# The last rows of an MLP: two products share banks, six half blocks leave VectorE, a pause in GpSimd's transfers

## What is computed

```python
proj = jnp.einsum('bsd,dc->bsc', x, w_in)          # 512 x 1024 times 1024 x 7680
y_a, y_b, y_c = conv(...), hgrn2(...), memory_attention(...)
merged = (sigmoid(ga + b_ga) * (y_a @ w_branch[0])
          + sigmoid(gb + b_gb) * (y_b @ w_branch[1])
          + sigmoid(gc + b_gc) * (y_c @ w_branch[2]))
x = layer_norm(ALPHA * x + merged @ w_o, ln1_g, ln1_b)
h = square(relu(x @ w_up))                          # 512 x 4096
x = layer_norm(ALPHA * x + h @ w_down, ln2_g, ln2_b)   # ALPHA = 2 ** 0.25
```

## Time and profile before

| | |
|---|---|
| median of three runs | 813.63 us (812.73 to 814.42) |
| the profiled execution | 814.37 us, of which the span from first to last instruction is 812.6 us |
| TensorE busy | 800.1 us (98%), granted clock 0.997 |
| VectorE, ScalarE, GpSimd busy | 552.5, 402.6, 117.2 us |

### The profile page before, as it was taken

The page is one execution under the profiler, slowest core; times in us unless marked ns, Lnnn a source line. Parts: engine busy times, 40 slices in busy tenths (PEclk is TensorE's granted clock), DMA queues, the critical chain, the costliest instruction groups (busy, mean ns, idle before and its releaser), DMA issues.

```text
span 812.6 us, 11668 instructions
## 1 busy us (share of the span) xinstructions
PE 800.1 (98%) x4779; PEld 711.4 (88%) x4779; DVE 552.5 (68%) x587; ACT 402.6 (50%) x457; POOL 117.2 (14%) x123
## 2 busy tenths in 40 slices
PE   8999999999999999999999999999999999999996
PEld 8889888889888888999998889887998899889984
DVE  4646645567367625878668677879378846985797
ACT  5559324494336232544454024672576348636934
POOL 1211112211111111111110115111101110000006
PEclk9999999999999999999999999999999999999998
DMA  8796868777776985885888668879998996456612
GB/s 302 225 342 221 203 108 188 178 134 113 235 240 181 229 226 113 228 212 86 285 303 276 112 102 235 204 175 247 336 296 232 279 241 216 161 204 243 224 52 104
DMA packets 81251, 168.45 MB, mean 207 GB/s; under 512 B 3341, under 2 KB 33078, under 8 KB 77622
## 3 DMA queue, kind: packets, MB, share of 16 engines
q1 hardware_dynamic: 58358, 109.08, 38.8%
q0 software_dynamic: 22848, 58.73, 35.7%
HBM read 165.70 MB, written 60.82 MB: 279 GB/s over the span
## 4 chain that ended last, share of the span: by engine, by line
PE 86%; DVE 8%; issue 2%; DMA 2%; ACT 1%; SPq 0%; DVEq 0%; ACTq 0%
PE bank L1989 28%; PE bank L1990 27%; PE bank L1991 27%; DVE w_lo L1256 2%; DVE two L1822 2%; DVE y_lo L1256 1%; DMA gate_c<-in_w_in_dram 1%; DMA two<-in_mem_dram 1%; DVE gate_b L1791 1%; DVE two L1791 1%; ACT w_hi L964 0%; PE bank L2205 0%; PE bank L2155 0%; PE bank L2016 0%; PE bank L2325 0%
## 5 line engine op out<-in xcount | busy, mean ns | idle before, releaser
L1989 PE MATMUL bank<-x_hi,w_hi 128*128 128x512 f32 (+1 forms) x624 | 211.8, 339 | 0.0
L1990 PE MATMUL bank<-x_lo,w_hi 128*128 128x512 f32 (+1 forms) x624 | 210.6, 338 | 0.0
L1991 PE MATMUL bank<-x_hi,w_lo 128*128 128x512 f32 (+1 forms) x624 | 210.6, 337 | 0.0
L1256 DVE TENSOR_TENSOR w_lo<-raw,w_hi 128x2048 fp32r<-128x2048 f32 (+2 forms) x51 | 108.1, 2121 | 37.2 <-ACT w_hi L1079 27.4
L1989 PEld LDWEIGHTS bank<-x_hi,w_hi 128*128 128x128 f32 x624 | 118.4, 190 | 12.5
L1991 PEld LDWEIGHTS bank<-x_hi,w_lo 128*128 128x128 f32 x624 | 118.4, 190 | 12.5
L1990 PEld LDWEIGHTS bank<-x_lo,w_hi 128*128 128x128 f32 x624 | 118.5, 190 | 12.2
L722 POOL DMA_DIRECT2D kept<-kept x56 | 64.5, 1153 | 362.9 <-issue 336.9
L1989 PE MATMUL bank<-w_hi,y_hi 128*128 128x512 f32 x296 | 115.7, 391 | 0.4 <-DVE two L1822 0.4
L1991 PE MATMUL bank<-w_hi,y_lo 128*128 128x512 f32 x296 | 115.2, 389 | 0.0
L1990 PE MATMUL bank<-w_lo,y_hi 128*128 128x512 f32 x296 | 115.2, 389 | 0.0
(11 more groups left out here) (278 smaller groups left out, 1395.0 us busy)
## 6 DMA issues: line engine op xcount, KB each, us to landing
kept<-kept POOLq DMA_DIRECT2D x56, 512.0 KB, 7.8
raw<-in_w_in_dram SPq DMA_DIRECT2D x22, 1024.0 KB, 7.5
raw<-kept SPq DMA_DIRECT2D x20, 1024.0 KB, 6.5
kept<-in_w_down_dram POOLq DMA_DIRECT2D x16, 1024.0 KB, 5.9
kept<-in_w_up_dram POOLq DMA_DIRECT2D x12, 1024.0 KB, 5.6
raw<-in_w_up_dram SPq DMA_DIRECT2D x8, 1024.0 KB, 7.8
raw<-in_w_down_dram SPq DMA_DIRECT2D x8, 1024.0 KB, 5.7
gate_a<-kept SPq DMA_DIRECT2D x8, 1024.0 KB, 6.5
```

What stands on the lines that cost most here:

```text
L1256: return dve.tensor_tensor(dst, src, high.bitcast(F32), ALU.subtract)
L1989: pe.matmul(dst, a[0], b[0], start=first, stop=False, skip_group_check=goes_on)
L1990: pe.matmul(dst, a[0], b[1], start=False, stop=False, skip_group_check=goes_on)
L1991: return pe.matmul(dst, a[1], b[0], start=False, stop=last, skip_group_check=goes_on)
```

## The change

1. **Last rows** (`LAST_ROWS`, `down_bank` gone): in group 3 both rows of m7 run before both rows of m4, and m4 accumulates on m7's banks. VectorE's second add of m7's bank (L1820, two instructions) is gone; a row of m4 now waits until VectorE has read m7's.
2. **Norm** (`SHARED`, `own_begin` and `own_end` gone): half block (0, 1) becomes the sixth that ScalarE and GpSimd make. SP stores it right after the fifth, ahead of block 1.
3. **Split moved**: the slab of group 3's down m7 is loaded and split right after the slab of up m4, five places earlier. It gets a place of its own in `x1_form_hi` and `x1_form_lo`. The gain and bias of the last norm land in other free places, and their loads wait for up m7 instead of up m3.
4. **Pause**: GpSimd makes the first step of jobs (2, 3) and then waits until both halves of gate 1's `gate_c` have landed before it issues the rest.
5. **Scaling**: GpSimd's four scalings by ALPHA are gone. The first add to each half block in group 0 (m1, m5, m6, m4: eight adds) is now `z * ALPHA + bank` in one instruction.

```diff
-SHARED = ((2, 0), (2, 1), (3, 0), (3, 1), (0, 0))
+SHARED = ((2, 0), (2, 1), (3, 0), (3, 1), (0, 0), (0, 1))
-LAST_ROWS = (("m6", 0), ("m3", 0), ("m6", 1), ("m3", 1), ("m7", 0), ("m4", 0), ("m7", 1), ("m4", 1))
+LAST_ROWS = (("m6", 0), ("m3", 0), ("m6", 1), ("m3", 1), ("m7", 0), ("m7", 1), ("m4", 0), ("m4", 1))
...
+    if aside(n, "m4"):
+        return at
+    if aside(n, "m7"):
+        return later + 1
+    return n if n < at else n + 1 if n < later else n + 2
...
-def down_bank(g, name):
-    return 2 if g == G_MLP - 1 and name == "m4" else ROW_BANK[name]
...
+            if aside(n, "m7"):
+                return tuple(f[:, 2:4, :].rearrange("p s t -> p (s t)") for f in (x1_form_hi, x1_form_lo))
...
+                        elif g == G_MLP - 1 and name == "m4":
+                            product_load("down", g, "m7")
-                for name in ROWS[0:6 if g == G_MLP - 1 else 7]:
+                for name in ROWS[0:5 if g == G_MLP - 1 else 7]:
                     if g == G_MLP - 1 and name == "m6":
-                        sp.wait_ge(mlp_done, slab_done(up_slab(g, "m3"), 1))
+                        sp.wait_ge(mlp_done, slab_done(up_slab(g, "m7"), 1))
...
             for n, (b, e) in enumerate(SHARED):
-                if n == 4:
-                    sp.wait_ge(y_ready, 1)
-                    store(0, 1)
                 sp.wait_ge(shared_ready, n + 1)
                 store(b, e)
             for e in range(2):
-                sp.wait_ge(y_ready, e + 2)
+                sp.wait_ge(y_ready, e + 1)
                 store(1, e)
...
-            make_sums((2, 3), range(4))
+            make_sums((2, 3), (0,))
+            pool.wait_ge(gate_c_landed, 32)
+            make_sums((2, 3), (1, 2, 3))
             begin_sums((4, 5))
             make_sums((4, 5), (0, 1))
-
-            for b in range(TB):
-                pool.wait_ge(aux_done, LNT.done("x%d1" % b))
-                pool.tensor_scalar(resid[:, b, :], resid[:, b, :], ALPHA, 1.0, ALU.mult, ALU.mult)\
-                    .then_inc(resid_ready, 1)
...
                 mlp_hi(up_slab(g, "m4"))
+                if g == G_MLP - 1:
+                    mlp_hi(down_slab(g, "m7"))
                 act.wait_ge(up_added, up_added_of(g, "m3", 1))
...
-                if g == G_MLP - 1 and name == "m7":
-                    z = half_of(b, 0)
-                    dve.tensor_tensor(z, z, bank[ROW_BANK[name] + r], ALU.add)
                 z = half_of(b, e)
-                dve.tensor_tensor(z, z, bank[down_bank(g, name) + r], op).then_inc(down_read, 1)
+                src = bank[ROW_BANK[name] + r]
+                if g == 0 and name in ("m1", "m5", "m6", "m4"):
+                    dve.scalar_tensor_tensor(z, z, ALPHA, src, ALU.mult, op).then_inc(down_read, 1)
+                else:
+                    dve.tensor_tensor(z, z, src, op).then_inc(down_read, 1)
...
                 complete("m7", 0)
+                complete("m7", 1)
                 complete("m4", 0)
                 moments(2, 0)
-                own_begin(2, 0, 1)
                 scales(2)
-                complete("m7", 1)
-                own_end(2, 0, 1)
                 complete("m4", 1)
                 norm_two(0, 1)
```

More of the change, by code:

```diff
@@ L117, in slab_done, with aside @@
     return 2 * n + p + 1
-def aside(n):
-    return n == down_slab(G_MLP - 1, "m4")
+def aside(n, name):
+    return n == down_slab(G_MLP - 1, name)
 def split_at(n):
-    at = up_slab(G_MLP - 1, "m2")
-    return at if aside(n) else n if n < at else n + 1
+    at, later = up_slab(G_MLP - 1, "m2"), down_slab(G_MLP - 1, "m1")
+    if aside(n, "m4"):
[3 more added lines that the diff above has]
+    return n if n < at else n + 1 if n < later else n + 2
 def row_done(g, name, r):
@@ L336, in build @@
         merged = small[:, 0:4096].rearrange("p (k t) -> p k t", k=KD)
-        ln_par = small[:, 4096:8192].rearrange("p (n d) -> p n d", n=4)
+        ln_par = small[:, 4096:6144].rearrange("p (n d) -> p n d", n=2)
+        ln2_par = small[:, 1024:2048], small[:, 5120:6144]
         late = small[:, 8192:9216].rearrange("p (c t) -> p c t", t=256)
@@ L484, in mlp_weights @@
         def mlp_weights(n):
-            return (aside_hi, aside_lo) if aside(n) else (w_hi[:, n % 3, :], w_lo[:, n % 3, :])
+            if aside(n, "m4"):
+                return aside_hi, aside_lo
+            if aside(n, "m7"):
+                return tuple(f[:, 2:4, :].rearrange("p s t -> p (s t)") for f in (x1_form_hi, x1_form_lo))
+            return w_hi[:, n % 3, :], w_lo[:, n % 3, :]
         def form_parts(g, name):
@@ L604, in _, with par_load @@
             branch_load(2, 1, seven_ring(2, "f1"), seven_slab(2, "m2"))
-            def par_load(n, v):
-                sp.dma_start(ln_par[:, n, :], v.to_broadcast((P, D))).then_inc(ln_landed, 16)
+            def par_load(to, v):
+                sp.dma_start(to, v.to_broadcast((P, D))).then_inc(ln_landed, 16)
             def out_load(n, free):
@@ L616, in _ @@
             sp.wait_ge(gate_done, seven_done(2, "m5", 1))
-            par_load(0, ln1_g)
-            par_load(1, ln1_b)
+            par_load(ln_par[:, 0, :], ln1_g)
+            par_load(ln_par[:, 1, :], ln1_b)
             x_reload(0, "m3")
@@ L770, in _ @@
                 pool.wait_ge(scaled, n + 1)
-                pool.tensor_tensor(resid[:, b, part], resid[:, b, part], ln_par[:, 2, part], ALU.mult)\
+                pool.tensor_tensor(resid[:, b, part], resid[:, b, part], ln2_par[0][:, part], ALU.mult)\
                     .then_inc(shared_step, 1)
                 pool.wait_ge(shared_step, n + 1)
-                pool.tensor_tensor(resid[:, b, part], resid[:, b, part], ln_par[:, 3, part], ALU.add)\
+                pool.tensor_tensor(resid[:, b, part], resid[:, b, part], ln2_par[1][:, part], ALU.add)\
                     .then_inc(shared_ready, 1)
@@ L1070, in mlp_hi @@
             def mlp_hi(n):
-                if aside(n):
+                if aside(n, "m4"):
                     act.wait_ge(mlp_done, slab_done(up_slab(G_MLP - 1, "m1"), 1))
+                elif aside(n, "m7"):
+                    act.wait_ge(mlp_done, slab_done(up_slab(G_MLP - 1, "m3"), 1))
                 elif n == 2:
@@ L1836, in scales @@
                 dve.reciprocal(last_norm[:, n, 2:3], last_norm[:, n, 1:2]).then_inc(scales_ready, 1)
[L1838 to L1849, removed]
             def norm_two(n, b):
@@ L1884, in seven_up @@
                 mlp_lo(up_slab(g, "m4"))
+                if g == G_MLP - 1:
+                    mlp_lo(down_slab(g, "m7"))
                 form_to_lo(g, "m2")
@@ L1935, in complete @@
                     half_stats(g, name, r)
-                mlp_lo(down_slab(g, "m7"))
                 form_to_lo(g, "m7")
@@ L2428, in row @@
                 down_ready(g, name, r)
-                opens = name in DOWN_OPENS or down_bank(g, name) != ROW_BANK[name]
+                opens = name in DOWN_OPENS
                 for j in range(PAIRS):
-                    mm = three(bank[down_bank(g, name) + r],
+                    mm = three(bank[ROW_BANK[name] + r],
                                tuple(f[:, j * 256 + r * P:j * 256 + (r + 1) * P] for f in form_parts(g, name)),
```

17 lines of the change are left out of this document (7 added, 10 removed).

## The result

| | before | after |
|---|---|---|
| median of 12 runs | 813.28 us (812.73 to 814.42) | 815.47 us (815.13 to 816.71) |
| the profiled execution | 814.37, span 812.6 | 815.49, span 813.6 |

The changed kernel is slower: ratio 1.0026, interval 1.0018 to 1.0034, which is +2.19 us.

What follows compares the result with a forecast made beforehand. It took TensorE's nearly unbroken matmul stream plus the tail behind it as the bound. Terms 1.9 + 0.1 - 1.4 + 0 = +0.6 took the profiled 814.37 to 815.0, so median 814.2 us; range 812.3 to 815.9.

Steps and rivals of the forecast that it cites:

- The last rows and the norm, +1.9: At the kernel's end: GpSimd's two more operations, started later, move the last three stores and the end by +1.9 us.
- GpSimd's tail does not decide: Rival on the kernel's end: only the gains count, -1.4 and -0.3, giving 811.9 us, faster; chance 0.13.
- my 794.3: At the norm near the end: predicted start of GpSimd's work on blocks 2 and 3, 1.4 us earlier than before.
- mutual hindrance: Rival on the end: GpSimd and VectorE slow each other, last four operations 0.8 us longer each, 817.3 us; chance 0.06.
- The pause, -1.4: At gate 1, near 324 us: `gate_c` lands 4.0 us sooner, closing TensorE's 1.12 us wait; -1.4 us, bounds 0 to 1.4.
- an offset of the profile: Whole kernel: the profiled 814.37 us lies 0.74 above the median 813.63, so forecast 815.0 becomes a median of 814.2.
- the pause brings nothing: Rival at gate 1: `gate_c`'s 8.87 us may be its own, so the 1.38 stays; 815.6 us, slower; chance 0.15.
- The split moved, +0.1: Group 3, before m3's first row: ScalarE's extra rounding makes VectorE 0.8 us late, costing +0.1 us, bounds 0 to 1.2.
- the rival of a stall: Rival at m3's slab: VectorE 1.9 us late, TensorE stops 1.2 us, 815.3 us, the edge of slower; chance 0.10.
- its cover of 0.6 to 0.8: At m3 in group 3: slack between the slab's low part, ending at 784.46, and TensorE's need; predicted just used up.
- The scaling, nothing: Near 500 us: VectorE gets back 3.1 us, but TensorE waits for nothing there, so no gain.
- +0.6: Sum for the whole kernel: 1.9 + 0.1 - 1.4 + 0, taking the profiled 814.37 to 815.0 us.

Runs made afterwards that it cites:

- the second profile of before: The kernel before, unchanged, profiled once more: 812.84 us, span 811.0.

## Why the forecast was right in sign and short in size

**The last rows and the norm, +1.9: right.** Compared with the second profile of before, from TensorE's last matmul to the end of the span there were 8.05 us (802.95 to 811.0), and now there are 9.84 (803.76 to 813.6): +1.79, and taking the two changes back gives 1.78. The chain was as foretold: VectorE's last add right behind TensorE's last row, GpSimd idle ahead of its ninth operation and last of all ahead of the stores. Its idle time of 1.44 us, not under one, came from an earlier start: 11.15 us ahead of TensorE's end (803.76 - 792.61), where my 794.3 was 10.2 ahead of 804.51. The rival by which GpSimd's tail does not decide is out (it ends 1.3 us behind VectorE), and so is the one of mutual hindrance: the last four operations took 1.26 to 1.27 beside VectorE's norm steps, whose second input is in PSUM. What the forecast did not see is how the two changes and the third share it. On its own the sixth half block costs 2.7, because GpSimd starts late; with the split moved GpSimd starts 2.3 earlier relative to TensorE's end, and it costs 0.2; the new row order then gives 1.6 away by making block 0's moments wait for the last row but one. The pause isn't what does it: with the pause alone GpSimd still starts 8.9 ahead. It is the slab. From the start of m5's adds to the first moments of the norm VectorE took 793.54 - 784.37 = 9.17 us before and 790.49 - 783.60 = 6.89 after, 2.28 less, and what is missing there is the low part of m7's slab (785.79 in the rows of the split below). The forecast had 1.4 for this, as it took VectorE's delay of 0.8 off; but TensorE stopped too, and m5's adds start 20.1 to 20.2 us ahead of its end in both profiles, so nothing was to be taken off.

**The pause, -1.4: the step that failed.** The forecast took the wait of 1.12 us from the one profile of before as a cost of every execution. In the second it is missing, and the pause is worth 0.1 to 0.3 in the median: 0.34 by adding it, 0.13 to 0.26 by removing it. The premise that the load has a benefit was right (4.6 to 5.1 us with the pause, 5.4 to 6.6 without, as medians of the two halves), and the part that nothing waits for GpSimd's later transfers held too: its next transfer behind the pause is at 308.61, its last issue at 675.17, and no wait of TensorE appeared between. A sign was there to be read. The profiled execution lay 0.74 above the median of the runs shown, and the forecast carried that difference on as an offset of the profile, although 1.38 of its time was exactly what the pause should save. The rival "the pause brings nothing", 815.6, came nearest to the measured 815.47, but not by its mechanism: `gate_c` did land faster, and the wait was simply not there to be saved.

**The split moved, +0.1: mis-sized.** It measured 0.57 as a stop and 0.72 by its undoing, inside the bounds of 0 to 1.2 and half of what the rival of a stall had, and what TensorE waits for was named wrongly. I followed the slab of m3 and its cover of 0.6 to 0.8. The adds of m5 are behind that slab on VectorE. Its timeline in the first profile of before, right behind the slab of the earlier trace rows:

```profile
784.37 1.50 DVE L1822 TENSOR_TENSOR two<-two,bank 128x512 f32<-128x512 f32 x2
785.79 2.29 DVE L1256 TENSOR_TENSOR w_lo<-raw,w_hi 128x2048 fp32r<-128x2048 f32 x1
```

The first add ended at 784.37 + 0.69 = 785.06, and TensorE started m3 at 785.29: a cover of 0.23 from end to start, of which 0.14 go between the two in any case. The add began 0.92 ahead of TensorE's start; in the changed kernel it begins 0.34 ahead of where the stream would have gone on (783.71 + 0.23 = 783.94). So VectorE is 0.6 later there, not 0.8, which the cover for the slab would have borne and the one for the add did not.

**The scaling, nothing: about -0.2.** VectorE's sums went back to the speed foretold. Its timeline in the changed kernel:

```profile
497.82 4.62 DVE L1754 TENSOR_TENSOR small<-x_hi,x_lo 128x1024 f32<-128x1024 f32 x4
```

4.62 instead of 8.01. The rule of the Trainium skill, "SBUF — State Buffer", section "Who interferes with whom", says that a VectorE instruction with two SBUF inputs contends with a GpSimd one that reads SBUF. The trace agrees: with GpSimd's scaling gone the sums of two SBUF operands take 1.16 us each instead of 2.0. None of that is gain, since nobody waits there. What is gained comes at the adds: TensorE's gap at 562 us is 0.55 from start to start (561.51 to 562.06) where the pause alone, without the scaling, has 0.74 (561.09 to 561.83). The gap is smaller by 0.2 in the profiles with the scaling changed; that it is the missing wait for the scaled half block which does it is argued only.

**The sum.** 1.8 + 0.6 - 0.2 - 0.3 = 1.9 (2.1 with the pause at 0.1), and 2.19 was measured, interval 1.5 to 2.8. The forecast's +0.6 lies outside that interval: the median fell into its range because the range was made wide enough for "the pause brings nothing", and not because its sum was near. Between the second profile of before and that of after the spans differ by 2.6. The tail has 1.8 of it. TensorE's end has 0.8, and of that the stop less the scaling is 0.4; the rest, 0.4, is there already when `gate_c` is issued (301.85 and 302.27), and at the start of the kernel too: `x_hi<-bank` stands at 21.02 and 21.45. That lies ahead of anything that was changed. Six further profiles of kernels with all of the split, the pause and the scaling have it at 21.3 to 21.7, the others at 21.0 to 21.4 but for the two late starts, so I can't say whether it is play between executions.

**What stays open.** Why `gate_c` lands late in some executions and not in others. The share of 14 in 99 is that of long runs and not of the wait: the wait of 1.12 us is shown in two profiles only, and one long run, with the pause, was late at the start instead. Why the first matmuls are slower in two of the profiles is open as well.

## What to carry to other kernels

Before a wait is priced, ask whether the profiled execution is an ordinary one: where it lies above the median, its own waits may be the reason, and they aren't there to be saved in the others. When work moves to another engine, look at when that engine can start and at which row releases its last block: here the sixth half block cost 2.7 us where GpSimd started late and 0.2 where it started early, and a row order that releases the last block later cost 1.6. When an instruction is late, check the cover of each one queued behind it, not only of the one that the change speaks of.

## What the runs showed of the hardware

- One load of 512 KB halves, in one place of one program, took 5.4 us in one profile and 6.6 in the other (median of two halves, the slower one 8.87), with GpSimd's transfer issued at the same time within 0.02 us. The Trainium skill, "DMA: Bandwidth & Descriptors", section "Issuing engines are not separate DMA queues", says that transfers of all issuers interleave on the 16 engines; the faster landing behind the pause agrees with that (4.6), and the play between executions is something that no number there gives.
- A matmul that starts behind a semaphore wait takes 0.47 us where its like takes 0.39, and the next starts 0.31 behind it where 0.23 is usual: each stop costs some 0.1 us beyond its gap, seen at 562, 566 and 784 us in several profiles.
- Three stores of 256 KB issued together end the span 3.8 us behind the first issue. One issued alone ended it 2.4 us behind where the store ahead of it had been issued 1.3 us earlier (808.43, block 1 first), and 3.0 us behind (809.05 to 812.0, half block (0, 1) last on VectorE) where that was 0.7 us (808.39).
